# Sample outputs of a recurrent mixer: states as the stationary operand, features on the partitions, head norm by a product with ones

## What is computed

```python
o_inter = (q * exp(b)) @ S          # GLA: 4 queries x state (64 x 128); retention: 4 queries x state (128 x 128)
o = o_inter + A @ v                 # A: decayed scores of the 4 tokens among themselves
o = o * rsqrt(mean(o * o, over the 128 features of the head) + EPS) * g * silu(gate)
```

## Time and profile before

| | us |
|---|---|
| median of 3 runs (lowest, highest) | 2246.22 (2245.95, 2246.39) |
| the profiled execution, its time | 2246.0 |
| its span, first to last instruction | 2244.2 |
| PE busy | 2217.3 |
| PEld busy | 2189.0 |
| DVE / ACT / POOL busy | 818.0 / 822.1 / 940.4 |

### The profile page before, as it was taken

One profiled execution on the slowest core, in us unless ns is written; L12 is line 12 of the kernel. 1 busy time (PEld: TensorE's weight loads), 2 busy tenths in 40 slices (PEclk: granted clock), 3 DMA queues, 4 the chain that ended last, 5 costly groups with the idle time before them and its releaser, 6 DMA issues.

```text
span 2244.2 us, 43741 instructions
## 1 busy us (share of the span) xinstructions
PE 2217.3 (99%) x17875; PEld 2189.0 (98%) x17875; DVE 818.0 (36%) x1150; ACT 822.1 (37%) x1445; POOL 940.4 (42%) x776
## 2 busy tenths in 40 slices
PE   8999999999999999999999999999999999999998
PEld 8999999999989999999999999999999899999998
DVE  5222200577367422220162222006863783222102
ACT  4333333442344433232353333335424453333333
POOL 3444444443315444444544444444432244444442
PEclk9999999999999999999999999999999999999999
DMA  6323222332234222323323322232221343322222
GB/s 172 91 84 90 76 85 85 89 84 76 67 83 141 76 84 84 93 69 91 112 70 90 88 84 74 87 95 78 82 75 49 94 130 94 92 86 82 78 88 74
DMA packets 382590, 197.60 MB, mean 88 GB/s; under 512 B 8868, under 2 KB 381400, under 8 KB 382360
## 3 DMA queue, kind: packets, MB, share of 16 engines
q1 hardware_dynamic: 365680, 186.93, 28.9%
q10 hardware_dynamic: 16808, 9.20, 1.4%
HBM read 186.80 MB, written 9.31 MB: 87 GB/s over the span
## 4 chain that ended last, share of the span: by engine, by line
PE 95%; DVE 3%; ACT 1%; issue 0%; DMA 0%; ACTq 0%; DVEq 0%
PE ps L544 88%; PE ps L719 1%; PE ps L879 1%; DVE x L1502 1%; DVE y L1496 1%; DVE xs_lo L1439 1%; PE ps L820 0%; PE ps L793 0%; PE ps L896 0%; PE ps L799 0%; PE ps L571 0%; PE ps L826 0%; ACT xs_hi L1069 0%; PE ps L760 0%; PE ps L822 0%
## 5 line engine op out<-in xcount | busy, mean ns | idle before, releaser
L479 POOL TENSOR_TENSOR w_lo<-raw,w_hi 128x512 fp32r<-128x512 f32 (+1 forms) x708 | 877.5, 1244 | 1150.5 <-ACT w_hi L1096 1150.4
L544 PE MATMUL ps<-xs_hi,w_hi 128*128 128x288 f32 (+1 forms) x3616 | 767.3, 289 | 4.4 <-DVE xs_lo L1439 4.2
L544 PE MATMUL ps<-xs_hi,w_lo 128*128 128x288 f32 (+1 forms) x3616 | 765.3, 288 | 0.0
L544 PE MATMUL ps<-xs_lo,w_hi 128*128 128x288 f32 (+1 forms) x3616 | 762.9, 288 | 0.0
L1096 ACT ACTIVATE w_hi<-raw 128x512 fp32r<-128x512 f32 (+1 forms) x708 | 409.9, 584 | 956.8 <-PE ps L544 956.0
L544 PEld LDWEIGHTS ps<-xs_hi,w_hi 128*128 128x128 f32 x3616 | 588.4, 189 | 11.0 <-DVE xs_lo L1439 6.2
L544 PEld LDWEIGHTS ps<-xs_lo,w_hi 128*128 128x128 f32 x3616 | 588.0, 189 | 0.2
L544 PEld LDWEIGHTS ps<-xs_hi,w_lo 128*128 128x128 f32 x3616 | 584.8, 188 | 0.0
L1460 DVE TENSOR_TENSOR tmp<-ps,rstd_pre 128x544 f32<-128x544 f32 x88 | 63.8, 725 | 630.2 <-PE ps L544 614.0
L544 PE MATMUL ps<-h_hi,w_lo 128*128 128x256 f32 x1272 | 267.2, 289 | 0.0
L544 PE MATMUL ps<-h_lo,w_hi 128*128 128x256 f32 x1272 | 266.1, 288 | 0.0
(11 more groups left out here) (214 smaller groups left out, 1874.1 us busy)
## 6 DMA issues: line engine op xcount, KB each, us to landing
raw<-in_w_gu_dram SPq DMA_DIRECT2D x176, 512.0 KB, 3.8
raw<-in_w_in_dram SPq DMA_DIRECT2D x56, 512.0 KB, 3.7
raw<-in_w_down_dram SPq DMA_DIRECT2D x64, 384.0 KB, 3.4
raw<-in_w_down_dram SPq DMA_DIRECT2D x64, 320.0 KB, 3.2
raw<-in_w_out_dram SPq DMA_DIRECT2D x16, 512.0 KB, 3.8
ret_state<-in_state_ret_dram SPq DMA_DIRECT2D x8, 512.0 KB, 6.0
out_dram<-ret_state ACTq DMA_DIRECT2D x8, 512.0 KB, 5.2
x_tok<-in_x_prompt_dram SPq DMA_DIRECT2D x4, 512.0 KB, 6.3
```

The costliest lines, as they stand in the source:

```text
L479: pool.tensor_tensor(lo, raw[:, u, k0:k0 + n, :], hi.bitcast(F32), ALU.subtract)\
L544: mm = pe.matmul(bank_part(bank, a), w, v[:, kx, TOK[a]], start=(start and n == 0), stop=(stop and n == 2))
```

## The change

`out_sample` exchanges the operands. The state (128 columns) is the stationary operand and the four queries of one sequence are the moving one; each product writes only its own four columns, and features lie on the partitions. The GLA queries are read as they are, the retention queries come from one small POOL operation, `decay_queries`, that waits for nothing but the tables. Squares, gates and root work on 128 partitions; the sum over the features is a product with a matrix of ones (`sample_sums`, ahead of k = 3). The gates are applied ahead of the root. `back(l, S)` is gone. On DVE `mask_values(l, 0)` moves behind `low_outputs(l, 2)`.

```diff
-    BACK_BANKS = ((2, 3), (5, 7), (1, 3), (5, 7), (1, 3))
-    BACK_S_AT = 6
+    BACK_BANKS = ((2, 3), (5, 7), (1, 3), (5, 7))
+    SUMS_S_AT = 3
+        SW = HA * TS
+        q_ret_s = acc[:, 0:HR * TS].rearrange("p (h t) -> p h t", t=TS)
+        def sample_out(gla, buf=None):
+            i0 = 0 if gla else HG // 2
+            if buf is None:
+                return ps[:, 0:3:2, i0 * TS:(i0 + HG // 2) * TS].rearrange("p a (i t) -> p a i t", t=TS)
+            b = buf[:, 0 if gla else HG:HG if gla else HA, :]
+            return b.rearrange("p (i a) t -> p a i t", a=2) if gla else b.rearrange("p (a i) t -> p a i t", a=2)
...
-            def mask_queries(l):
+            def decay_queries(l):
                 pool.wait_ge(tables_loaded, 16)
-                wait(pool, o_ready, l, NCH - 2)
                 pool.sem_inc(mask_begun, 1)
-                pool.memset(acc[:, :], 0.0)
-                pool.memset(v_tok[:, 0], 0.0).then_inc(q_zeroed.sem, 1)
-                wait(pool, q_zeroed, l, 0)
...
-                        o = pool.tensor_tensor(
-                            dst[:, :, at:at + nb * step_].rearrange("p h (b t) -> p h b t", b=nb)[:, :, :, 0:DS],
-                            src[:, :, t0:t0 + nb * DS].rearrange("p h (b t) -> p h b t", b=nb),
-                            scale.broadcast_to([P, n, nb, DS]), ALU.mult)
-                o.then_inc(q_masked.sem, 1)
+                pool.tensor_tensor(q_ret_s.rearrange("p h (b t) -> p h b t", t=DS),
+                                   q_r[:, :, TP:T].rearrange("p h (b t) -> p h b t", t=DS),
+                                   q_decay.broadcast_to([P, HR, NS, DS]), ALU.mult).then_inc(q_masked.sem, 1)
...
             def out_sample(l, heads):
-                    return ps[0:TS, BANK0[S] + 2 * a, i * DV:(i + 1) * DV]
+                    return ps[:, 2 * a, i * TS + at.start:i * TS + at.stop]
                 for h in heads:
-                    pe.matmul(place(h), a_gla_s[:, h % 2, h // 2, :] if h < HG else a_ret_s[:, h - HG, :],
-                              v_gla_s[:, h, :] if h < HG else v_ret_s[:, h - HG, :], start=True, stop=False)
+                    pe.matmul(place(h, slice(0, TS)), v_gla_s[:, h, :] if h < HG else v_ret_s[:, h - HG, :],
+                              a_gla_s[:, h % 2, h // 2, :] if h < HG else a_ret_s[:, h - HG, :], start=True, stop=False)
                 for b in range(NS):
+                    at = slice(b * DS, (b + 1) * DS)
                     for h in heads:
...
-                            queries, state = q_ret_s[:, h - HG, b * TS:(b + 1) * TS], ret_state[:, h - HG, b, :]
-                        mm = pe.matmul(place(h), queries, state, start=False, stop=(b == NS - 1))
+                            state, queries = ret_state[:, h - HG, b, :], q_ret_s[:, h - HG, at]
+                        mm = pe.matmul(place(h, at), state, queries, start=False, stop=(b == NS - 1))
+            def sample_sums(l):
+                wait(pe, k_low, l, 0)
+                wait(pe, o_sq, l, S)
+                pe.matmul(ps[:, 3, 0:SW], ones, sq[:, 0, 0:SW], start=True, stop=True).then_inc(o_ms.sem, 1)
...
-                        if k0 + k == BACK_S_AT:
-                            back(l, S)
+                        if k0 + k == SUMS_S_AT:
+                            sample_sums(l)
...
+            def square_sample(l):
+                wait(act, o_ready, l, S)
+                for gla in (True, False):
+                    o = act.activation(sample_out(gla, sq_sample), sample_out(gla), ACT.Square)
+                o.then_inc(o_sq.sem, 1)
+            def root_sample(l):
+                wait(act, o_ms, l, S)
+                act.activation(sq[:, 1, 0:SW], ps[:, 3, 0:SW], ACT.Ln, bias=eps, scale=1.0 / DV).then_inc(o_log.sem, 1)
+                wait(act, o_log, l, S)
+                act.activation(sq[:, 1, 0:SW], sq[:, 1, 0:SW], ACT.Exp, scale=-0.5).then_inc(o_root.sem, 1)
...
-                act_step(l, "squares", S)
-                act_step(l, "root", S)
+                square_sample(l)
+                root_sample(l)
...
+            def gate_sample(l):
+                v = v_t[:, :, TP:T]
+                wait(dve, o_sq, l, S)
+                for gla in (True, False):
+                    o = dve.tensor_tensor(sample_out(gla, v), sample_out(gla), sample_out(gla, g_t[:, :, TP:T]), ALU.mult)
+                o.then_inc(sample_gated.sem, 1)
+                wait(dve, sample_gated, l, 0)
+                wait(dve, o_root, l, S)
+                dve.tensor_tensor(v, v, rstd_sample, ALU.mult)\
+                   .then_inc(o_gated.sem, 1)
...
                 low_outputs(l, 0)
+                low_outputs(l, 1)
+                gate_sample(l)
+                low_outputs(l, 2)
                 mask_values(l, 0)
-                low_outputs(l, 1)
-                dve_step(l, "squares", S)
-                dve_step(l, "root", S)
-                dve_step(l, "back", S)
-                low_outputs(l, 2)
                 mask_values(l, 1)
```

More of the change, by code:

```diff
@@ L233, in trunk_kernel @@
         sb("h_place", [P, 2 * KF * T])
-        QW = NS * TS
-        q_gla_s = acc[:, 0:QT * QW].rearrange("p (q t) -> p q t", t=QW)
-        q_ret_s = v_tok[:, 0].rearrange("p h v -> p (h v)")[:, 0:HR * QW].rearrange("p (h t) -> p h t", t=QW)
+        SW = HA * TS
[6 more added lines that the diff above has]
+            return b.rearrange("p (i a) t -> p a i t", a=2) if gla else b.rearrange("p (a i) t -> p a i t", a=2)
+        sq_sample, rstd_sample = (sq[:, n, 0:SW].rearrange("p (h t) -> p h t", t=TS) for n in range(2))
         def v_by_batch(i):
@@ L317, in trunk_kernel @@
         turned, v_tok_ready, k_tok_ready = sig("turned", NSTEP + 1), sig("v_tok_ready", NCH), sig("k_tok_ready", NCH)
-        qd_ready, q_zeroed, q_masked = sig("qd_ready", NCH - 1), sig("q_zeroed", 1), sig("q_masked", 1)
+        qd_ready, sample_gated, q_masked = sig("qd_ready", NCH - 1), sig("sample_gated", 1), sig("q_masked", 1)
         ret_scores, a_ret_ready = sig("ret_scores", NSTEP), sig("a_ret_ready", NSTEP)
@@ L321, in trunk_kernel @@
         o_ready, o_sq, o_ms = sig("o_ready", NSTEP), sig("o_sq", NSTEP), sig("o_ms", NSTEP)
-        o_log, o_root, o_normed = sig("o_log", NSTEP), sig("o_root", NSTEP), sig("o_normed", NSTEP)
-        o_turned, o_gated = sig("o_turned", NSTEP), sig("o_gated", NSTEP - 1)
+        o_log, o_root, o_normed = sig("o_log", NSTEP), sig("o_root", NSTEP), sig("o_normed", NCH)
+        o_turned, o_gated = sig("o_turned", NCH), sig("o_gated", NSTEP - 1)
         first_copied, first_gated = sig("first_copied", 1), sig("first_gated", 1)
@@ L525, in _ @@
                         spread_sample(l)
-                        mask_queries(l)
+                        decay_queries(l)
                         group(l * GROUPS + WOUT, FULL_KT)
@@ L838, in back @@
                     wait(pe, in_read, l, NIN - 2)
-                elif c_ < S:
+                else:
                     wait(pe, state_ready, l, c_)
@@ L842, in back @@
                         wait(pe, a_ret_ready, l, S)
-                else:
-                    wait(pe, k_low, l, 0)
                 for h in range(HA):
                     a, i = out_slot(h)
-                    mm = pe.transpose(ps[:, BACK_BANKS[c_][h // 4], h % 4 * n:(h % 4 + 1) * n],
-                                      o_tok[0:n, 4 * a + i, :], ident[0:n, 0:n])
+                    mm = pe.transpose(ps[:, BACK_BANKS[c_][h // 4], h % 4 * CH:(h % 4 + 1) * CH], o_tok[:, 4 * a + i, :], ident)
                 mm.then_inc(o_turned.sem, 1)
@@ L862, in out_sample, with place @@
                     wait(pe, a_ret_ready, l, S)
[L864 removed]
+                def place(h, at):
                     a, i = out_slot(h)
[L867 removed]
+                    return ps[:, 2 * a, i * TS + at.start:i * TS + at.stop]
                 for h in heads:
[L870 to L871 removed]
+                    pe.matmul(place(h, slice(0, TS)), v_gla_s[:, h, :] if h < HG else v_ret_s[:, h - HG, :],
+                              a_gla_s[:, h % 2, h // 2, :] if h < HG else a_ret_s[:, h - HG, :], start=True, stop=False)
                 for b in range(NS):
+                    at = slice(b * DS, (b + 1) * DS)
                     for h in heads:
@@ L875, in out_sample @@
                             rows = slice(h % 2 * DKG, (h % 2 + 1) * DKG)
-                            queries, state = q_gla_s[rows, h // 2, b * TS:(b + 1) * TS], gla_state[rows, h // 2, b, :]
+                            state, queries = gla_state[rows, h // 2, b, :], q_dec[rows, h // 2, TP + at.start:TP + at.stop]
                         else:
-                            queries, state = q_ret_s[:, h - HG, b * TS:(b + 1) * TS], ret_state[:, h - HG, b, :]
-                        mm = pe.matmul(place(h), queries, state, start=False, stop=(b == NS - 1))
+                            state, queries = ret_state[:, h - HG, b, :], q_ret_s[:, h - HG, at]
```

(5 more changed lines are left out.)

1 line of the change is left out of this document (removed).

## The result

The changed kernel takes 2273.44 us (median of 4 runs, 2272.77 to 2274.22); the kernel before, run beside it, 2246.30 (4 runs, 2245.95 to 2246.87). The ratio is 1.012, with a 95% interval of 1.0108 to 1.0133: the changed kernel is 27 us slower. The forecast was 2270, in a range of 2244.5 to 2275.

The account below looks back on a forecast made before the run. PE bounds the kernel, busy 2217.3 of 2244.2 us. Terms of +0.15, -0.34 and -0.2 give -0.4 us a layer (2245.2 us); with the clock fall +12.6 a layer, 2271, put at 2270, range 2244.5 to 2275.

Parts of the forecast that it names:

- The work only moves from the moving side to the load: PE's products with states: loads set the pace at 112 ns a record, +0.03 us a head, +0.15 us a layer.
- Turning back against the sum: PE's output projection: eight transposes (0.80 us) go, a ones product (0.46) comes, -0.34 us a layer; a gap before it, -0.2.
- The cover of the new waits: PE's waits for squares and split sample outputs stay hidden, with 1 us of cover and over 1 us earlier: no cost.
- POOL earlier, "nothing": POOL's splits of output weights begin near 635 instead of 644.65; PE doesn't use them before 667.6, so no effect.
- The clock: Stretch with states: PE moves almost nothing, so its clock halves from 655.5, +11.2 us a layer before recovery; chance 0.54.
- The way back: Recovery of PE's clock after the stretch with states: 3.7 us of work at half pace, 1.8 us lost a layer.
- The delay of 2.6 us at the end: End of the earlier trace: the clock fell 2.6 us after PE's last work near 2240; used to time the fall.
- The sum per layer: All terms with the clock fall, per layer: +12.6 us, +25 in all, giving 2271.
- The rival with a staying clock: PE's clock stays at 1.00 through the stretch with states: 2245.2 us, 2243.5 to 2247; chance 0.38.

Follow-up runs that it names:

- last_narrow: contig128 with the last retention head moving its own 4 columns a state product, as in the changed kernel: 2250.62 us, ratio 1.0020 to the kernel before.
- contig128: Changed kernel, each state product moving 128 columns (32 masked queries four times over) into four output copies side by side: 2248.26 us, ratio 1.0007 to the kernel before.
- the dose series: Changed kernel with 16, 32, 64 or 128 columns moved per state product instead of 4: 2273.22, 2271.39, 2263.76, 2248.05 us.

## Why the prediction was right, and where it was off

The direction and the mechanism held; the forecast was 3.4 us too low. That the time lies in the range says little, since the range took in the clock that stays (2245.2) as well as the one that falls; the claim that could fail was the fall itself, held at 0.54, hardly more than an even chance.

- **The work only moves from the moving side to the load**: held. A head was taken as 16 x 112 ns and a gap of 0.1, 1.89 us, and measured 1.88 at the full clock (last_narrow): +0.02 us instead of +0.03.
- **Turning back against the sum**: the sum was taken as 0.46 us and measured 0.43 at the full clock (contig128, its L899, below). The first pair of tiles with what stands in it takes 12.48 us there and took 13.03 before (4.46, 0.61 and 7.96): 0.55 less, where 0.34 and 0.2 were forecast. The gain was there, hidden under the clock.

```profile
668.68 2.15 PE ps L556 x18
670.83 0.43 PE ps L899 x2
671.26 9.90 PE ps L556 x78
```

- **The cover of the new waits**: held. PE doesn't wait for the squares or for the low parts. At half clock it had more time still.
- **POOL earlier, "nothing"**: wrong. PE doesn't use the split weights sooner, but POOL's work beside DVE's product of chunk 2's queries makes that last 1.25 us and not 0.68, and PE waits 0.5 us a layer. I had asked what the earlier weights free, and not what their making collides with. It is 1.1 us of the result.
- **The clock**: the open question, whether loading counts as work, was put at 0.54 for no; the dose series shows no. The sizes came out partly by luck. The fall was taken at 655.5; it came at 653.6 in layer 0, and in layer 1 2.8 us into the stretch (1776.6 against 1773.86), about as taken. All work was taken to last twice as long at half clock; a retention head took 3.50 us against 1.88, 1.86 times as long. So what is lost ahead of the output projection, taken as 11.2 us, was some 11.4 in layer 0, where the early fall and the smaller factor cancel, and 10.0 in layer 1. The way back was taken as 3.7 us of work at half pace; it took 4.7 in layer 0 (679.66 to 684.4) and 5.5 in layer 1 (1798.49 to 1804.0). The row it was sized from, the transposes at the start, shows long durations only: the granted clock reads 1.00 there. The delay of 2.6 us at the end was 2.4, since PE's last work ended at 2240.03.
- **The sum per layer**: 12.6 foreseen, 13.2 and 12.1 measured. Against the kernel before beside it, 27.1 us were measured and 24 forecast: 25.3 are these two stretches, 1.1 is POOL's, and 1 of the 3 missing is the rounding down from my own sum of 2271.
- **The rival with a staying clock** can be priced from the rows. Put each piece of the two stretches that ran at half clock at its length at the full clock (1.88 for a head or pair, 1.06 for the transposes, 0.33 for two records of scores with values as in the kernel before, 2.15, 0.43 and 9.90 from contig128, 0.44 for the wait that then shows). They shrink by some 13.7 and 12.6 us, to 27.2 each, against 27.6 before. So, by this estimate, the clock cost 26 us and the rest of the change gains 0.4 to 0.5 a layer, as the prediction had it; with POOL's 1.1 this rival is some 2246.5. No kernel ran that has 4 columns and the full clock throughout, so it stays an estimate.

Still open: what part the wait ahead has in the early fall of layer 0 (in the profiles it came between 653.1 and 656.0 with up to 64 columns moved), and why 128 loaded and 128 moved columns take 124 ns together here where either long side by itself gives 116 to 117.

## What to carry to other kernels

Count what PE moves, not only how long it is busy: exchanging operands so that a matrix is loaded for four columns moved would have saved about 1 us at the full clock, and cost some 26 through the clock. When one side is narrow, leave it stationary and give every product output partitions of its own, so that four run side by side; then look at once for the engine that is late next, since a wait of 3.9 us cost clock as well. And when an instruction is freed to run earlier on POOL, look at what DVE reads from SBUF at that time.

## What the runs showed that I had not expected

- With 64 columns moved for each load of 128 the clock still fell: 2263.8 us, and the two runs lay 9.5 us apart.
- Products on four sets of 32 output partitions ran four at a time even with all 128 rows in use: 64 records in 1.96 us, 31 ns each.
- One DVE product of 128x512 with both operands in SBUF: 0.68 us alone, 1.25 beside POOL's subtraction.
